# Three places for arriving weights and four for split ones, in a kernel that streams its weights

## The reference

```
S, D_MODEL, DEPTH = 256, 1024, 2
def first_block(x, ...):
    for layer in range(DEPTH):
        h = rms_norm(x, norm_gain[layer])
        proj = h @ w_in[layer]                  # 1024 x 9304
        ...  # q, k, v, gates of two branches
        y_a = dsa_attention(q_a, k_a, v_a, q_i, k_i, w_i) * silu(z_a)
        o_b = chunked_gated_delta_rule(q_b, k_b, v_b, beta, g)
        y_b = rms_norm(o_b, gdn_norm_gain[layer]) * silu(z_b)
        mixed = gates[:, :, 0, :] * y_a + gates[:, :, 1, :] * y_b
        x = x + mixed @ w_out[layer]
    return rms_norm(x, final_gain)

def second_block(x, mem, ...):
    for l in range(DEPTH):
        h = x @ w_in[l]                         # 1024 x 3620
        ...  # latent, stick-breaking, forgetting and memory attention: y_0 .. y_3
        for n in range(4):
            merged += sigmoid(merge_r @ w_merge_up)[n] * ((y_n * silu(gate_z[n])) @ w_branch[n])
        x = layer_norm(ALPHA * x + merged @ w_out[l])

out = second_block(first_block(x, ...), mem_2, ...)
```

## Time and profile before

| | |
|---|---|
| median of 3 runs | 1161.22 us (1160.76 to 1161.28) |
| the profiled execution | 1163.95 us |
| its span in the profile | 1162.1 us |
| PE busy | 1086.8 us, 94% |
| DVE busy | 684.2 us, 59% |
| POOL busy | 668.7 us, 58% |
| ACT busy | 585.9 us, 50% |
| TensorE clock granted, mean | 0.979 of full speed |
| bytes moved | 152.07 MB, 131 GB/s on the mean |

### The profile page before, as it was taken

How to read it: one execution, slowest core, us unless ns; L and a number is a source line. 1 busy time by engine, 2 the same in 40 slices (tenths; PEclk the granted TensorE clock), 3 DMA queues, 4 the chain that set the end, 5 groups by cost and what they waited for, 6 DMA issues and landing times.

```text
span 1162.1 us, 17023 instructions
## 1 busy us (share of the span) xinstructions
PE 1086.8 (94%) x6482; PEld 948.4 (82%) x6482; DVE 684.2 (59%) x1213; ACT 585.9 (50%) x861; POOL 668.7 (58%) x288
## 2 busy tenths in 40 slices
PE   5989999999989999999999998899999879999986
PEld 4978999888868898889988887787887667897865
DVE  3666655787495547546676477506646652665554
ACT  4535145745553465333656275345566433457651
POOL 3746445564466766444765364687445874744584
PEclk9999999999998999999999999999999988999999
DMA  8634334452415554333454332474433554543351
GB/s 277 180 110 141 94 108 118 118 148 78 120 51 196 163 158 143 111 108 110 131 160 127 82 117 93 145 215 121 125 91 109 181 163 145 139 123 107 93 181 55
DMA packets 84447, 152.07 MB, mean 131 GB/s; under 512 B 10576, under 2 KB 16528, under 8 KB 84368
## 3 DMA queue, kind: packets, MB, share of 16 engines
q1 hardware_dynamic: 84368, 151.00, 43.6%
HBM read 149.93 MB, written 1.05 MB: 130 GB/s over the span
## 4 chain that ended last, share of the span: by engine, by line
PE 79%; DVE 10%; ACT 5%; issue 2%; POOL 2%; DMA 1%; POOLq 0%; DVEq 0%; SPq 0%; ACTq 0%
PE bulk L900 43%; PE bulk L888 11%; PE chain L977 10%; PE chain L921 4%; ACT arena L1278 2%; PE bulk L893 2%; POOL w_lo L837 2%; PE chain L1238 1%; PE chain L959 1%; PE chain L1102 1%; ACT w_hi L1278 1%; ACT L1273 1%; PE chain L1219 1%; DVE arena L1758 1%; DVE arena L1671 1%
## 5 line engine op out<-in xcount | busy, mean ns | idle before, releaser
L837 POOL TENSOR_TENSOR w_lo<-raw,w_hi 128x1024 fp32r<-128x1024 f32 (+4 forms) x279 | 654.4, 2361 | 471.5 <-ACT w_hi L1278 471.0
L1278 ACT ACTIVATE w_hi<-raw 128x1024 fp32r<-128x1024 f32 (+4 forms) x279 | 280.1, 1016 | 250.2 <-PE bulk L900 207.8
L900 PE MATMUL bulk<-w_hi,hT_hi 128*128 128x512 f32 (+1 forms) x756 | 308.9, 409 | 13.2 <-DVE arena L1758 7.9
L900 PE MATMUL bulk<-w_hi,hT_lo 128*128 128x512 f32 (+1 forms) x756 | 296.1, 392 | 0.0
L900 PE MATMUL bulk<-w_lo,hT_hi 128*128 128x512 f32 (+1 forms) x756 | 295.6, 391 | 0.0
L900 PEld LDWEIGHTS bulk<-w_hi,hT_hi 128*128 128x128 f32 x756 | 143.6, 190 | 47.8 <-DVE arena L1758 10.7
L900 PEld LDWEIGHTS bulk<-w_hi,hT_lo 128*128 128x128 f32 x756 | 143.0, 189 | 30.4
L900 PEld LDWEIGHTS bulk<-w_lo,hT_hi 128*128 128x128 f32 x756 | 143.8, 190 | 26.7 <-issue 1.2
L977 PE MATMUL chain<-arena 128*128 128x128 f32 x1056 | 131.3, 277 | 5.6 <-ACT arena L1278 3.6
L977 PEld LDWEIGHTS chain<-arena 128*128 128x128 f32 x1056 | 126.2, 192 | 11.3 <-issue 3.9
L888 PE MATMUL bulk<-hT_hi,w_hi 128*128 128x256 f32 x384 | 112.0, 292 | 0.0
(11 more groups left out here) (244 smaller groups left out, 1378.4 us busy)
## 6 DMA issues: line engine op xcount, KB each, us to landing
raw<-in_w_in_dram SPq DMA_DIRECT2D x194, 512.0 KB, 3.6
raw<-in_w_out_dram SPq DMA_DIRECT2D x32, 512.0 KB, 4.4
raw<-in_w_branch_dram SPq DMA_DIRECT2D x16, 512.0 KB, 3.8
raw<-in_w_mem_kv_dram SPq DMA_DIRECT2D x8, 512.0 KB, 3.8
raw<-in_w_merge_up_dram SPq DMA_DIRECT2D x16, 256.0 KB, 2.7
raw<-in_w_in_dram SPq DMA_DIRECT2D x8, 420.0 KB, 3.3
gain<-in_ln_rows_dram SPq DMA_DIRECT2D x4, 512.0 KB, 5.2
gain<-in_gains_dram SPq DMA_DIRECT2D x3, 512.0 KB, 6.5
```

Source lines behind the costliest of these rows:

```text
L837: pool.tensor_tensor(lo_of(p, u)[:, 0:n], raw_of(p, u)[:, 0:n], hi_of(p, u)[:, 0:n].bitcast(F32), ALU.subtract).then_inc(p.done("split"), 1)
L900: m = pe.matmul(dst, a, b[:, k, :], start=(first and k == 0 and i == 0), stop=(last and k == nk - 1 and i == 2))
L1278: return act.activation(dst, src, func, **more)
```

## The change

The kernel has five raw places of 4 KB in each partition and three split places of 8 KB, 44 KB together. Afterwards it has three and four, again 44 KB. IN_ST and IN_HT are numbered behind the ring, so their numbers move from 3 and 4 to 4 and 5. The second edit is in `tile_in`: ACT waited for the unit of a tile with the highest number and now waits for the one that `in_turn` lists last in the order in which PE multiplies. The two differ for one tile only, h1 of layer 1 of block two, whose units are multiplied in another order for each half of the rows.

```
@@ -151,8 +151,8 @@
-RAW_SLOTS = 5
-SPLIT_SLOTS = 3
+RAW_SLOTS = 3
+SPLIT_SLOTS = 4
 IN_ST, IN_HT = SPLIT_SLOTS, SPLIT_SLOTS + 1
 LOOK = 3
@@ -1294,7 +1294,7 @@
                 def tile_in(name):

-                    last = max(u for u, x in enumerate(UNITS[p.sec]) if x[0] == name)
+                    last = in_turn(p.sec, p.l, name, R - 1)[-1]
                     act.wait_ge(*o.after("tensor", *last_mm(p.sec, p.l, last)))
                     return bulk_of(p, name), dict(TILES[p.sec])[name]
```

## The result

The changed kernel takes 1178.7 us (median of 4 runs, 1175.44 to 1180.13) against 1160.99 us (4 runs) of the kernel before: a ratio of 1.0152, with a 95% interval of 1.0131 to 1.0173. It is slower, as forecast, by 17.7 us where 6.4 were forecast, and it lies above the range (1160.0 to 1174.0). The profiled execution took 1180.13 us, the slowest of the four, with a span of 1178.3, 16.2 more than before.

What follows compares the result with a forecast made beforehand. The prediction took TensorE (PE), busy 94% of the span, as the bound. Terms (1) to (6) lost 9.8 us, (7) to (9) gained 3.4: +6.4 on 1161.2 gave 1167.6 us, range 1160.0 to 1174.0.

Steps and rivals of the forecast that it cites:

- (1): End of block two, layer 0: unit 226's later load delays ACT's copy and DVE's hT_lo; PE 2.4 us late (1.8 to 3.6).
- (2): End of layer 1: unit 283's load waits for POOL's split of unit 280; 0.9 us lost (0.4 to 2.4).
- (3): The start: unit 7's load now stands behind the parameter and gain loads; 0.3 us lost (0 to 1).
- (4): Block one, layer 1, norm and mix chain: moved POOL splits stop L2117 and L2126, delaying PE's transposes; 3.0 us lost.
- (5): Block one, layer 0, same chain: POOL splits moved onto small DVE operations and L2117; 1.6 us lost (0 to 2.4).
- (6): Layer 1: block one's key norm and delta rule scales, block two's latent norm; 0.7 + 0.5 + 0.4 = 1.6 us lost.
- (7): Block two's first norm: a later raw load moves a POOL split back, so scale L2317 runs unblocked; 1.6 us gained.
- (8): Norm ahead of block two: the POOL split beside the second L1671 moves 2.7 us forward; 1.0 us gained (0 to 1.5).
- (9): ACT's queue is blocked less often by a waiting split, shortening PE's L959 waits; 0.8 us gained (0 to 1.1).
- the starved case: Rival, whole stream: landings grow to 4.7 us, disturbances reach PE, three more stalls add 7.1 us; 1174.7 us, chance 0.13.
- The estimate of 3.2 us: Skill's landing time for a 512 KB load; by it (1) would be 1.3, (2) nothing, and the time 1165.6 us.

Runs made afterwards that it cites:

- the held splits: Changed kernel with ACT splits of 14 units (76 to 79, 131 to 134, 162 to 167) also waiting for PE's last matmul three units back: 1165.38 us.

## Why the prediction was wrong in size

The direction, the mechanism and most of the places were right. POOL's splits did move under DVE's chains, and three raw places did cost at the start and at the ends of block two's layers. By steps, with what the matmuls' start times of the two profiled executions show:

- (1) End of block two, layer 0: taken 2.4, came 3.8, of which 2.0 was the gap and 1.7 matmuls at half clock behind it; 0.5 was won back within 7 us. ACT's copy began at 949.38 behind a split that had waited 2.32 us for its load, as worked out.
- (2) End of layer 1: taken 0.9, came 0.4. (3) Start: taken 0.3, came 1.5, with a gap of 1.19 for POOL's w_lo; the loads ahead of unit 7's were issued only at 27.7 to 29.3 us and not beside the others. Terms 1 to 3 less gain 7 gave 2.0; three raw places alone cost 4.8.
- (4) Mix chain, layer 1: taken 3.0, came 3.6 of gap and 2.6 of slow matmuls, 5.1 in the run that takes it away. The mechanism was right step for step up to the gap.
- (5) Mix chain, layer 0: taken 1.6, came 1.8 in the trace; 3.5 is left by difference in the runs, which its uncertainty lets stand beside 1.8.
- (6) Three further places: taken 1.6 together. The scales of the delta rule alone, taken at 0.5, came to 2.8 at 584.63 (a gap of 2.65), and 4.7 in the run that takes it away; the key norm came to nothing for 0.7. At the latent norm 1.8 came for 0.4, but by another operation than forecast: PE waited (1.69 us) for L2182 of the stick-breaking attention, two operations on 128x1024 that took 5.42 us beside POOL where they had taken 1.94. Here the step failed that priced each of these places at "up to one split". It counted one moved split where two now followed each other, and each split of a row stops one more dependent operation. The rows for it were there: L1833, L1836 and L1838 beside three splits near 70 us. I had not read them.
- (7) and (8), the gains: taken 1.6 and 1.0, came 2.0 and 1.2. (9) taken 0.8, came 0.8 (PE's waits at L959 are 1.2 of 2.0).
- No term at all was there for TensorE's clock. PE's busy time grew by 5.2 us, 2.6 of it behind the gap of (4) and 1.7 behind that of (1). Every term gave a gap its own length. Against a miss of 9.8 in the profiled executions (16.2 for 6.4), these two places are 4.3, and the undercount of (6) is 3.0.

The three places of the held splits were in the sum, at 3.0 + 1.6 + 0.5 = 5.1 us; the run that takes them away gave 13.3. The chance given to the starved case, 0.13, held a time near the measured one, 1174.7, for a wrong reason: PE's waits for POOL's w_lo grew by 2.5 us in all, not by 7.1, and its premise, slower landings, did not come. Loads of 512 KB from w_in and from w_out both landed in 3.6 us on the median in the changed kernel. The estimate of 3.2 us that the prediction names beside it is not borne out either. The Trainium skill, DMA: Bandwidth & Descriptors, "Anatomy of one DMA", gives that fit for DMAs that GpSimd issues, and here SP issues them.

## What to carry to other kernels

The deeper buffer did nothing here for a bound engine that was never short, but it moved work in time, and the work that moved shut another engine out. Before lengthening a ring, list the dependent chains of small operations on the path and see what the freed work would run beside; price a meeting by the number of long instructions in a row times their length, and allow for a half-clock stretch behind each new gap of TensorE of some 3 us (1.5 to 2.6 us in four traces). Compare two traces only with a third one of equal code at hand: here a pause of 0.2 us moved 2.6 us between executions. Where the order of two engines decides, a wait on the side with time to spare (three waits, -7.7 us) is worth more than a buffer.

## What the runs showed of the hardware

- A DVE operation of 128x4 elements, both inputs in SBUF, waits a full POOL split (2.25 us for 0.16), and so does a TENSOR_SCALAR with one input tensor, L1833 (128x8, 2.38 for 0.17). A TENSOR_SCALAR of two elements in each partition took 1.85 us beside a split (L2152, kernel before, 1006.87). One of one element was not stopped, though it began 0.1 us after a POOL split had; the TENSOR_TENSOR behind it was (DVE of the changed kernel, block two's first layer norm; the same in nine other traces):

```profile
966.97 0.15 DVE L1599 TENSOR_SCALAR tiny<-tiny 128x1 f32<-128x1 f32 x1
967.15 2.08 DVE L1601 TENSOR_TENSOR tiny<-tiny 128x1 f32<-128x1 f32 x1
```

- Behind a gap of PE of 2.83 us (an added DVE operation) and of 3.43 us (the changed kernel) the granted clock stood at 0.50 for 3 and 5.5 us and then rose; the matmuls behind the gap cost 1.5 and 2.6 us beyond the gap itself.
- A gap alone does not settle it. One of 2.87 us near 710 us and one of 2.6 to 2.7 us near 926 us (in the kernel before's time) stand in all twelve traces, and half clock follows each of them in eight; near 190 us it comes without a long gap just ahead. What decides stays open, and it makes executions of one program differ.
